# Convolution moved between score levels, four modulation tiles summed on VectorE: a two-layer hybrid decoder trunk on one Trainium2 core

## The reference, cut to what matters

```
mod = silu(c) @ mod_w + mod_b                       # (2, 6*1024): 2 layers x 12 tiles of 512 columns
h = rms_norm(x) * (1 + scale) + shift
proj = h @ w_in                                     # 13 weight tiles of 1024 x 512
q, f_raw, i_val, g_out, z, xbc, dt_raw = split(proj)
o_a = hgrn2_chunk_scan(...)                         # causal scores with decay, 8 heads
xbc = silu(causal_dwconv(xbc, conv_w, conv_b))      # 4 taps, 1536 channels
y = ssd_chunk_scan(xs, dt, a, bm, cm) + d_skip * xs # 16 heads
x = x + gate * (concat(norm(o_a) * silu(g_out), norm(y * silu(z))) @ w_out)
x = x + gate * grouped_moe(h)                       # then layer 1: RWKV-7 mixer, the same MoE
```

## Time and profile before

| | us |
|---|---|
| median of 3 runs | 1223.91 (1222.65 to 1224.27) |
| the profiled execution, its time | 1220.31 |
| its span in the profile | 1218.6 |
| TensorE busy in it | 1147.1 (94%) |
| VectorE busy | 431.5 (35%) |
| ScalarE busy | 269.7 (22%) |
| granted TensorE clock, mean | 0.969 |

### The profile page before, as it was taken

The page is one execution under the profiler, slowest core; times in us unless marked ns, Lnnn a source line. Parts: engine busy times, 40 slices in busy tenths (PEclk is TensorE's granted clock), DMA queues, the critical chain, the costliest instruction groups (busy, mean ns, idle before and its releaser), DMA issues.

```text
span 1218.6 us, 15728 instructions
## 1 busy us (share of the span) xinstructions
PE 1147.1 (94%) x6533; PEld 751.5 (62%) x6533; DVE 431.5 (35%) x946; ACT 269.7 (22%) x444; POOL 93.4 (8%) x107
## 2 busy tenths in 40 slices
PE   4799999998989999999999699989999999999996
PEld 2686698984478844444455378838878744444553
DVE  0364754265720511111111484884432511111113
ACT  2222110414220411111111353323330411111113
POOL 5002221200000100000000001341000100000000
PEclk9999899999989899999999799998999899999999
DMA  9787765339966389959999521000069589999990
GB/s 351 267 325 276 276 230 184 139 103 380 402 244 251 138 289 387 387 185 387 387 387 341 215 94 44 1 0 2 2 232 389 207 324 387 387 387 387 387 363 35
DMA packets 157180, 309.56 MB, mean 254 GB/s; under 512 B 9568, under 2 KB 10940, under 8 KB 157116
## 3 DMA queue, kind: packets, MB, share of 16 engines
q1 hardware_dynamic: 156320, 307.39, 69.4%
q10 hardware_dynamic: 796, 1.23, 0.3%
HBM read 307.55 MB, written 1.05 MB: 253 GB/s over the span
## 4 chain that ended last, share of the span: by engine, by line
PE 85%; DVE 6%; SPq 3%; ACT 2%; DMA 1%; issue 1%; ACTq 1%; DVEq 0%
PE bank L1147 19%; PE bank L792 15%; PE bank L1171 10%; PE bank L853 7%; PE bank L1079 6%; PE bank L1071 6%; PE bank L803 2%; PE bank L916 2%; DVE scratch L2420 2%; PE bank L825 1%; PE bank L1204 1%; DVE arena L1976 1%; PE bank L1212 1%; PE bank L1383 1%; DVE scratch L2422 1%
## 5 line engine op out<-in xcount | busy, mean ns | idle before, releaser
L792 PE MATMUL bank<-arena,ring 128*128 128x256 f32 x960 | 211.5, 382 | 5.7 <-DMA ring<-in_ev_w_in 3.0
L792 PEld LDWEIGHTS bank<-arena,ring 128*128 128x128 f32 x960 | 182.7, 191 | 31.0 <-DMA ring<-in_ev_w_in 3.4
L1147 PE MATMUL bank<-ring,arena 128*64 128x512 f32 x704 | 153.7, 592 | 0.0
L1147 PEld LDWEIGHTS bank<-ring,arena 128*64 128x64 f32 x704 | 50.4, 137 | 99.6 <-issue 99.4
L2293 DVE TENSOR_TENSOR arena<-arena,bank 128x512 f32<-128x512 f32 x17 | 11.7, 688 | 220.7 <-PE bank L1147 220.7
L853 PE MATMUL bank<-arena,ring 128*128 128x256 f32 x384 | 85.0, 385 | 2.9 <-issue 2.9
L1079 PE MATMUL bank<-arena 128*128 128x256 f32 x336 | 84.6, 400 | 1.7 <-issue 1.7
L1147 PE MATMUL bank<-arena 128*64 128x512 f32 x384 | 84.1, 592 | 0.0
L853 PEld LDWEIGHTS bank<-arena,ring 128*128 128x128 f32 x384 | 74.1, 193 | 13.6 <-issue 3.2
L1071 PEld LDWEIGHTS bank<-arena 128*128 128x128 f32 x608 | 69.3, 192 | 13.8 <-issue 13.8
L1071 PE MATMUL bank<-arena 128*128 128x128 f32 x608 | 72.7, 278 | 0.0
(11 more groups left out here) (362 smaller groups left out, 1322.1 us busy)
## 6 DMA issues: line engine op xcount, KB each, us to landing
ring<-in_moe_w SPq DMA_DIRECT2D x112, 1024.0 KB, 14.2
arena<-in_moe_w SPq DMA_DIRECT2D x80, 1024.0 KB, 14.2
ring<-in_mod_w SPq DMA_DIRECT2D x24, 2048.0 KB, 11.2
ring<-in_ev_w_in SPq DMA_DIRECT2D x13, 2048.0 KB, 13.0
ring<-in_od_w_rkv SPq DMA_DIRECT2D x6, 2048.0 KB, 13.6
ring<-in_ev_w_out SPq DMA_DIRECT2D x4, 2048.0 KB, 17.3
ring<-in_od_w_o SPq DMA_DIRECT2D x2, 2048.0 KB, 10.3
arena<-in_x ACTq DMA_DIRECT2D x1, 1024.0 KB, 9.4
```

What stands on the lines that cost most here:

```text
L792: mm = pe.matmul(ps[:, c * S:(c + 1) * S], w_cols(slot)[:, k, (2 * half + c) * P:(2 * half + c + 1) * P], src[:, k, :], start=(k == 0), st ...
L1147: mm = pe.matmul(bank[4 + half][e * C:(e + 1) * C, :], hgT[:, kb, e * C:(e + 1) * C], piece(slots[e], kb), start=(kb == 0), stop=(kb == KB ...
```

## The change

Three things are moved.

1. The convolution goes on VectorE in between the score levels: blocks 8, 9, 10 at level 3, blocks 11, 0, 1 at level 4, blocks 2, 3 at level 5, blocks 4 to 7 at level 6, always between `level_mult` and `level_take`. Its SiLU on ScalarE goes in front of the gate's evacuation.
2. Layer-1 modulation tiles 12 to 15 are summed on VectorE where the convolution stood, into four accumulators in buffer 7. TensorE turns them into columns behind the transposes L982, in place of its four `modulation` calls among the HGRN2 outputs.
3. Tiles 4 to 11 are summed earlier, so that VectorE has none after level 2: tile 5 before the forget gates, tiles 6, 7 and 8 before the diagonal scores are taken, tiles 9, 10, 11 at levels 0, 1, 2. `mod_direct` follows: tiles 4, 5 behind projection 4, then 6, 7 and 8, 9 and 10 and 11 behind projections 5 to 8.

```diff
-            for m in range(5, 7):
+            for m in range(6, 9):
                 mod_sum(m)
...
             for i in range(8):
                 level_mult(i)
-                for m in range(7 + i, min(8 + i, MOD_DVE)):
+                for m in range(9 + i, min(10 + i, MOD_DVE)):
                     mod_sum(m)
+                for b in between.get(i, ()):
+                    conv(b)
                 if i < 7:
                     level_take(i)
...
-            for b in range(XBLK):
-                tmp = ctmp[:, b % 2, :]
...
+            for m in range(MOD_DVE, MOD_LATE):
+                mod_sum(m)
             dve.wait_ge(dtN_full, 1)
...
+            between = {3: (8, 9, 10), 4: (11, 0, 1), 5: (2, 3), 6: (4, 5, 6, 7)}
...
-                for m in {4: (4, 5), 5: (6,), **{n: (n + 1,) for n in range(6, 11)}}.get(n, ()):
+                for m in {4: (4, 5), 5: (6, 7), 6: (8, 9), 7: (10,), 8: (11,)}.get(n, ()):
                     mod_direct(m)
...
                 mm.then_inc(o_full, 1)
-                modulation_step()
...
                 mm.then_inc(xs_full, 1)
+            for m in range(MOD_DVE, MOD_LATE):
+                mod_direct(m)
             pe.wait_ge(xdt_ready, 3)
...
             level_exp(7)
+            act.wait_ge(conv_done, XBLK)
+            act.activation(xpad[:, :, TAPS - 1:], xpad[:, :, TAPS - 1:], ACT.Silu).then_inc(conv_silu, 1)
             act.wait_ge(mod_full, MOD_DVE)
             evac_T(gT, 0, ACT.Silu)
```

More of the change, by code:

```diff
@@ L64 @@
 MOD_DVE = 12
+MOD_LATE = 16
 NSUB = 4
@@ L355, in trunk, with mod_acc @@
         slide = [buf(i)[:, 2 * W:2 * W + KB * 63].rearrange("p (k n) -> p k n", k=KB) for i in (10, 1)]
-        MOD_GROUPS = ((0, MOD_FIRST), (MOD_DVE, 24))
+        MOD_GROUPS = ((0, MOD_FIRST), (MOD_LATE, 24))
         def mod_group(m):
             return [g for g, (a, b) in enumerate(MOD_GROUPS) if a <= m < b][0]
-        mod_acc = [buf(10)[:, i * W:(i + 1) * W] for i in (0, 1, 3, 2)]
+        mod_acc_early = [buf(10)[:, i * W:(i + 1) * W] for i in (0, 1, 3, 2)]
+        mod_acc_late = [buf(7)[:, i * W:(i + 1) * W] for i in range(4)]
+        def mod_acc(m):
+            return (mod_acc_early if m < MOD_DVE else mod_acc_late)[m % 4]
         def mod_slot(m):
@@ L530, in wait_used @@
                 at = places[l, kind].index(n)
-                if kind == "mod" and MOD_FIRST <= 12 * l_mod + j < MOD_DVE:
+                if kind == "mod" and MOD_FIRST <= 12 * l_mod + j < MOD_LATE:
                     sp.wait_ge(mod_summed, 12 * l_mod + j + 1 - MOD_FIRST)
@@ L832, in mod_direct @@
                 for q in range(4):
-                    mm = pe.matmul(bank[6][:, 4 * m + q:4 * m + q + 1], mod_acc[m % 4][:, q * P:(q + 1) * P],
+                    mm = pe.matmul(bank[6 if m < MOD_DVE else 1][:, 4 * m + q:4 * m + q + 1],
+                                   mod_acc(m)[:, q * P:(q + 1) * P],
                                    ones[:, 0:1], start=True, stop=True)
                 mm.then_inc(mod_full, 1)
-            mod_next = [MOD_DVE]
+            mod_next = [MOD_LATE]
             def modulation_step():
                 if mod_next[0] < 24:
-                    if mod_next[0] == 12:
+                    if mod_next[0] == MOD_LATE:
                         pe.wait_ge(basics, 3)
@@ L1660, in _ @@
                 act.activation(dst(fT), bank[6 + u % 2][:], ACT.Square).then_inc(o_evac, 1)
-            act.wait_ge(conv_done, XBLK)
-            act.activation(xpad[:, :, TAPS - 1:], xpad[:, :, TAPS - 1:], ACT.Silu).then_inc(conv_silu, 1)
             for u in range(4):
@@ L1931, in mod_sum @@
                 slot, count = mod_slot(m)
-                acc = mod_acc[m % 4]
+                acc = mod_acc(m)
                 dve.wait_ge(tile_landed[slot], 16 * count)
-                dve.wait_ge(mod_full, max(MOD_FIRST, m - 3))
+                if m < MOD_DVE:
+                    dve.wait_ge(mod_full, max(MOD_FIRST, m - 3))
                 link(ts_(acc, w_cols(slot)[:, 0, :], csilu[:, 0:1], None, ALU.mult))
@@ L1998, in _ @@
             mod_sum(MOD_FIRST)
+            mod_sum(MOD_FIRST + 1)
             dve.wait_ge(proj_evac, 4)
@@ L2040, in level_take, with conv @@
                     ins.then_inc(score_evac, 1)
+            def conv(b):
+                dve.wait_ge(proj_evac, 14 if b >= KB else 16 if b < 4 else 18)
+                tmp = ctmp[:, b % 2, :]
+                wt = lambda j: col("ev_conv_w", j * XBLK + b)
+                link(ts_(tmp, xpad[:, b, 0:S], wt(0), col("ev_conv_b", b), ALU.mult, ALU.add))
+                for j in range(1, TAPS - 1):
+                    link(stt(tmp, xpad[:, b, j:j + S], wt(j), tmp, ALU.mult, ALU.add))
+                stt(xpad[:, b, TAPS - 1:], xpad[:, b, TAPS - 1:], wt(TAPS - 1), tmp, ALU.mult,
+                    ALU.add).then_inc(conv_done, 1)
+            between = {3: (8, 9, 10), 4: (11, 0, 1), 5: (2, 3), 6: (4, 5, 6, 7)}
             level_diff(0)
             level_diff(1)
-            for m in range(5, 7):
+            for m in range(6, 9):
                 mod_sum(m)
@@ L2084, in _ @@
             gains(0, 1)
-            dve.wait_ge(proj_evac, 18)
-            for b in range(XBLK):
-                tmp = ctmp[:, b % 2, :]
[L2089 to L2094, removed]
+            for m in range(MOD_DVE, MOD_LATE):
+                mod_sum(m)
             dve.wait_ge(dtN_full, 1)
@@ L2121, in _ @@
             normed = count[0]
+            dve.wait_ge(mod_full, MOD_LATE)
             def decay_diff(h):
@@ L2159, in _ @@
             dve.wait_ge(mod_cols, 2)
-            modulation(1, 0, 48, bank[2]).then_inc(mod_taken, 1)
+            modulation(1, 4 * MOD_LATE - 48, 48, bank[2])
+            dve.wait_ge(mod_full, MOD_LATE)
+            tt_(modT[:, 1, 0:4 * MOD_LATE - 48], bank[1][:, 48:4 * MOD_LATE], cols("mod_b", 48, 4 * MOD_LATE),
+                ALU.add).then_inc(mod_taken, 1)
             dve.wait_ge(mod_taken, 3)
```

## The result

The changed kernel takes 1239.63 us (median of 4 runs, 1239.03 to 1243.96) against 1224.09 before: a ratio of 1.0134, with a 95% interval of 1.0101 to 1.0167. Run again beside the experiments it gave 1239.76 (1235.79 to 1243.96), ratio 1.0136. The forecast was 1230.7, with a range to 1234.5: the sign was right, but 6.8 us more were forecast and 15.5 came.

What follows compares the result with a forecast made beforehand. The prediction took TensorE, busy for 94% of the span, as the bound up to 270 us, then a chain passing between engines. +5.8 (diagonal scores) and +1.0 (tail) made +6.8 on 1223.91: 1230.7 us, range 1224.5 to 1234.5.

Steps and rivals of the forecast that it cites:

- the sum of tile 8: VectorE's sum ahead of taking the diagonal groups: waits for `mod_direct(4)` until 111.5 us, then runs to 117.4.
- the moved `mod_direct`: One-column matmuls of tiles 4 to 11, regrouped behind projections 4 to 8: no cost of their own in the sum.
- the low clock in the tail: Thin TensorE work after the output steps: half clock there would cost 4.0 us, bounds nothing to 7.1.
- The sum ahead of the diagonal scores: Tile 8's sum delays the diagonal groups and level 0 scores: +5.8 us (3.9 to 7.8), order plus clock.
- +3.9 us from the order: Level 0 scores start at 122.1 us, not 118.25, because VectorE waits before tile 8's sum.
- +1.9 from the clock: Low clock already during the two remaining diagonal groups, after a longer TensorE idle stretch: +1.9 us, bounds nothing to +3.9.
- The tail: Output steps to products and sums: 3.0 us gained at full clock, 4.0 lost to low clock, +1.0 net.
- The estimate made in the prediction from the Trainium skill: Tail at half clock for about 10 us, costing 5 us: tail +2.0, forecast 1 us later.
- The convolution at the levels: Convolution blocks on VectorE at levels 3 to 6: costed at nothing, with 7.6 us for level 6's four blocks.
- rival 3: VectorE bounds the levels: convolution at level 6 holds the level 7 scores, 2 us more, 1232.7; 5%.
- rival 4: Modulation tiles 16 to 23 come late for the heads, some 2 us, 1232.7; 3%.
- Rivals 1 and 2: 1: order's cost only, clock adds nothing, +0.9, 1224.8, 18%. 2: no low clock after diagonal scores, 1219.7, 6%.

Runs made afterwards that it cites:

- experiment 1: Changed kernel with an accumulator of its own (buffer 11) for tile 8, whose sum no longer waits for `mod_direct(4)`: 1227.69 us.
- experiment 2: Changed kernel with tile 8 summed behind `level_mult(0)`, in front of the sum of tile 9: 1225.56 us.
- experiment 9: Changed kernel in which GpSimd starts its level 1 product of keys only after the sum of tile 8 has ended: 1236.85 us.
- experiment 10: Changed kernel with the edits of experiment 2 and Experiment 3 together, tiles 12 to 15 still summed on VectorE: 1226.12 us.
- Experiment 3: Changed kernel with the one-column matmuls where they stood before, one tile behind each of projections 5 to 10: 1237.98 us.
- experiment 4: Kernel before the change with 32 more dense 128x256 matmuls behind projection 2, as a pure delay: 1236.61 us.

## Why the prediction was wrong

The waits and their order were right. Three steps of the sum were too small or missing: the length of the sum of tile 8, taken as 5.9 us, was 8.4; the moved `mod_direct` was put at nothing and shows 3.3 us; and the low clock in the tail, taken as 4.0 us, took 6.3.

**The sum ahead of the diagonal scores: right in mechanism, too small.** The prediction had +3.9 us from the order and +1.9 from the clock here. VectorE's sum started at 111.06 as worked out (111.5, less 0.48), and the two diagonal groups took 3.79 us instead of 1.92. What I had not seen is that GpSimd's product of keys runs at 112.68 and holds the sum up by 2.4 us: I took the sum's length from a row in which GpSimd was idle. Measured +8.2 at the level 0 scores, +7.7 behind the next projection, against +5.8. Experiments 1 and 2 show the wait, experiment 9 the 2.4 us. The +1.9 of the clock came out as worked out, but experiment 10 shows that the low clock in this place does not come in every execution.

**The moved `mod_direct`: costed at nothing, wrong, and the largest of the three misses.** This term is missing from the sum. Two tiles behind projections 5 and 6 make the stretch of thin matmuls (one and 64 columns) longer, and the clock falls there with TensorE busy: +3.3 us by the rows. I had looked for the low clock only where TensorE would idle. Experiment 3 shows the stretch at full clock and 3.1 us less by 272 us; by the medians it gives 1.7 us, within the spread.

**The tail: the term was mis-sized.** I took +1.0, with bounds of -3.0 and +4.1; it is +3.3 (43.1 against 39.8 us). The order was as worked out: output steps in 5.8 us, first xdt 24.4 us after the copies of level 7. The clock was the error: it took 6.3 us and not 4.0. Against their prices at full clock the rows have 3.3 us more in the four tiles, 0.4 in the transposes, 1.2 in the products and 1.3 in the sums. The estimate made in the prediction from the Trainium skill (TensorE: Matmul & The Clock Gate, Part 1) was 5, nearer to that than my value.

**The convolution at the levels: right, with a surprise that cost nothing.** At level 6 its four blocks took 13.1 us and not 7.6, again beside GpSimd. The first of its rows in VectorE's timeline of the changed kernel, and the copy of the level's scores that follows them:

```profile
245.11 2.44 DVE L2056 TENSOR_SCALAR scratch<-arena,vcols 128x256 f32<-128x256 f32 x1
...
258.18 1.34 DVE L2047 COPY_PREDICATED arena<-level,bank 128x512 f32<-128x512 int32 x2
```

The scores of level 7 stand at 265.12, so rival 3 did not come. Nor did rival 4: from 311 to 330 us, among the heads, the distance to the kernel before stays at 14.35 us. Rivals 1 and 2 needed a full clock and had none.

**Sum.** 7.7 + 3.3 + 0.5 (small pieces up to 265 us) + 3.3 is 14.8 us at the end of the sums, less the 0.48 by which this execution was ahead: 14.3, as the rows show (308.24 - 293.90). The medians lie 15.5 apart. The 5.4 us by which the first profile is longer still are low clock in layer 1, which the second profile of the same kernel does not have. Why the clock falls there in some executions is open: a delay of 15.0 us did not bring it on (experiment 4), nothing here shows what does, and that the change makes it more frequent is not ruled out. The terms above are therefore those of the rows up to 310 us. That their sum of 14.3 lies so near the 15.5 of the medians is in part luck: without the wait of tile 8 (experiment 2) the median is already within 1.4 us of the kernel before, where the rows leave some 6.

One sum in the prediction does not come out: the range that it gives the forecast as its own, +2.5 to +11.9, should begin at +0.9 by its own bounds (3.9 - 3.0). The stated range is not built on it.

## What to carry to other kernels

Before work is moved into an engine's idle time, look for the semaphore that it waits on: idle time ahead of a wait for a later event is no room, and what is queued behind pays. Take a VectorE duration from a row in which GpSimd does what it will do beside it. And count a run of one-column or narrow matmuls as a place where the low clock can begin, even when TensorE is never idle; keep such matmuls apart, between dense ones. Here this was worth 3.3 us in the rows, and in the medians less than the spread of the runs lets one tell.

## What the runs showed of the hardware

A VectorE instruction with two SBUF tensors waited out a GpSimd one: 0.76 us became 3.17 beside a GpSimd product of 3.10 us. Seven in a row took 7.88 us (tile 8) and 8.96 us (tile 10, from 149.35 us) in the changed kernel and 9.45 us in experiment 1, instead of 5.48. With GpSimd moved away those of tile 8 took 5.48 again. The Trainium skill (GPSIMD Engine Reference, 1. Specifications) says that GpSimd shares its SBUF interfaces with VectorE and contends with VectorE instructions that have two SBUF inputs; the runs agree. A convolution instruction with one tensor input was also slowed, 2.44 us instead of 0.41 (first block of level 6): it ended at 247.55, and a GpSimd product of 3.39 us beside it at 247.40.

The granted clock fell to 1.2 GHz in stretches where TensorE was busy for all of the time: in the changed kernel it was 1.00 from 150 to 152 us and 0.50 from 154 to 156. It fell between the two, towards the end of 6.2 us of one-column and 64-column matmuls (147.94 to 154.09). And 2.1 us of idle TensorE in front of the level 0 scores were followed by 0.51 from 118 to 128 us in the kernel before and by 1.00 in the same ten microseconds of experiment 10.
